# HGRN levels of a two-layer encoder: one product a chunk for both directions, with K kept as a row in use and another row

## What is computed

```python
def gates(f):                      # once for each direction
    log_f = logaddexp(log(lb), log1p(-lb) + log_sigmoid(heads(f)))
    k = (1 - lb) * sigmoid(-heads(f))
    return log_f, k

def step(state, (qc, kc, vc, lfc)):          # a chunk of a head
    b = cumsum(lfc, axis=2)
    o_inter = (qc * exp(b)) @ state
    decay = where(lower, exp(b[t] - b[s]), 0)     # for each t, s, feature
    scores = einsum('tk,sk,tsk->ts', qc, kc, decay)
    o = scores @ vc + o_inter
    state = exp(b_last) * state + (kc * exp(b_last - b)).T @ vc
```

## Time and profile before

| | |
|---|---|
| median of 3 runs | 2987.6 us (2986.75 to 2990.24) |
| the profiled execution | 2987.38 us, its span 2985.6 us |
| granted TensorE clock, mean | 0.957 of full |
| PE busy | 2762.4 us (93%) |
| DVE busy | 1412.0 us (47%) |
| HGRN levels, from the first to turn_k of the last head | 1382.96 to 2092.77 us |

### The profile page before, as it was taken

One profiled execution on the slowest core, in us unless ns is written; L12 is line 12 of the kernel. 1 busy time (PEld: TensorE's weight loads), 2 busy tenths in 40 slices (PEclk: granted clock), 3 DMA queues, 4 the chain that ended last, 5 costly groups with the idle time before them and its releaser, 6 DMA issues. The chain is left out here.

```text
span 2985.6 us, 36800 instructions
## 1 busy us (share of the span) xinstructions
PE 2762.4 (93%) x14372; PEld 2332.0 (78%) x14372; DVE 1412.0 (47%) x2483; ACT 551.4 (18%) x809; POOL 620.4 (21%) x448
## 2 busy tenths in 40 slices
PE   6686699999999999978999999999799999999996
PEld 5575577788888888767888888889678888888885
DVE  8599416533332322544555655556483332333326
ACT  3222313111111111121222222221211111111110
POOL 3868311111112111111111111110011111111120
PEclk8798799999999999989999999997899999999998
DMA  4233214111111111011101011000411111111101
GB/s 134 70 104 94 68 44 168 57 43 56 42 42 45 54 56 43 29 56 36 29 22 35 21 35 28 21 21 0 169 37 49 56 56 42 47 52 42 42 14 57
DMA packets 207704, 158.01 MB, mean 53 GB/s; under 512 B 15616, under 2 KB 189824, under 8 KB 206720
## 3 DMA queue, kind: packets, MB, share of 16 engines
q1 hardware_dynamic: 207616, 156.81, 17.2%
HBM read 139.02 MB, written 17.76 MB: 53 GB/s over the span
## 5 line engine op out<-in xcount | busy, mean ns | idle before, releaser
L588 DVE TENSOR_TENSOR h<-h,ps 128x512 f32<-128x512 f32 x320 | 219.5, 686 | 199.9 <-PE ps L365 199.6
L347 PE MATMUL ps<-aT_hi,w_hi 128*128 128x512 f32 x704 | 278.5, 396 | 3.2 <-DVE aT_lo L561 3.2
L347 PE MATMUL ps<-aT_hi,w_lo 128*128 128x512 f32 x704 | 276.4, 393 | 0.0
L347 PE MATMUL ps<-aT_lo,w_hi 128*128 128x512 f32 x704 | 274.2, 389 | 0.0
L1728 PE MATMUL ps<-aT_hi,w_hi 128*128 128x512 f32 x640 | 257.2, 402 | 1.7 <-PEq L241 1.7
L1728 PE MATMUL ps<-aT_hi,w_lo 128*128 128x512 f32 x640 | 251.3, 393 | 0.0
L1728 PE MATMUL ps<-aT_lo,w_hi 128*128 128x512 f32 x640 | 250.0, 391 | 0.0
L1762 PEld LDWEIGHTS ps<-hg_q_decayed,hg_k_decayed 128*128 128x128 f32 x1792 | 227.2, 207 | 6.2 <-DVE hg_k_decayed L2041 2.8
L1762 PE MATMUL ps<-hg_q_decayed,hg_k_decayed 128*128 128x64 f32 x1792 | 225.6, 289 | 2.6 <-DVE hg_k_decayed L2041 2.6
L1700 POOL TENSOR_TENSOR w_lo<-w_raw,w_hi 128x1024 fp32r<-128x1024 f32 x38 | 94.4, 2493 | 639.1 <-ACT w_hi L62 639.1
L571 DVE TENSOR_TENSOR s5o_act_out<-s5o_act_out,ps 128x512 f32<-128x512 f32 x44 | 30.2, 687 | 350.7 <-ACT s5o_act_out L460 350.7
(11 more groups left out here) (313 smaller groups left out, 5957.6 us busy)
## 6 DMA issues: line engine op xcount, KB each, us to landing
w_raw<-in_ffn_w_in_dram SPq DMA_DIRECT2D x44, 512.0 KB, 5.1
w_raw<-in_hg_w_in_dram SPq DMA_DIRECT2D x40, 512.0 KB, 3.9
s5o_raw<-in_ffn_w_in_dram SPq DMA_DIRECT2D x22, 512.0 KB, 5.1
s5o_raw<-in_ffn_w_out_dram SPq DMA_DIRECT2D x11, 1024.0 KB, 5.2
hgo_raw<-in_ffn_w_in_dram SPq DMA_DIRECT2D x22, 512.0 KB, 5.0
hgo_raw<-in_ffn_w_out_dram SPq DMA_DIRECT2D x11, 1024.0 KB, 5.0
h<-in_x_dram SPq DMA_DIRECT2D x4, 1024.0 KB, 8.9
s_w_raw<-in_s_w_in_dram SPq DMA_DIRECT2D x8, 512.0 KB, 4.8
```

Source lines behind the costliest of these rows:

```text
L347: ins = t.matmul(ps[:, 2 * b + a, :], w[q][:, a, kk, :], x[:, kk, rows], start=(kk == 0 and m == 0), stop=(kk == KT - 1 and m == 2))
L588: v.tensor_tensor(part, part, ps[:, 4 + m % 4, :], ALU.add).then_inc(S["out_acc"], 1)
```

## The change

`Q` of both directions becomes one tile, `q_both` (named hg_q_decayed), with the backward row first and the forward row 1024 elements behind it. `K` becomes three rows: `k_used[0]`, `k_used[1]` and `k_other`. The row in use holds, at each position, the K (forward or backward) that this level multiplies; `k_other` holds the K of the other direction at that position. One product a chunk then serves both directions: it loads the chunk of the row in use and streams 128 columns, which `q_used` gathers block by block, alternately from the backward and the forward row. The result is a full 128x128 square in natural order over banks 2 and 3.

From one level to the next half of the positions change their direction. So DVE copies the middle two of every four blocks from `k_other` into the row that comes next, and multiplies the four quarters of the row in use by their block totals, two into the next row and two into `k_other`; the last level has halves for quarters. This stands ahead of the wait for the products; then come the two Q instructions, and one masked copy of 1024 elements. PE waits for `level_moved` (Q done) and for `level_kept` (the masked copy done) before the next level. `start_k` on ACT writes in four strided instructions of 512.

```diff
-    Q = [sb(f"q_decayed{d}", [P, T]) for d in range(2)]
-    K = [sb(f"k_decayed{d}", [P, T]) for d in range(2)]
+    q_both = sb("q_decayed", [P, 2 * T + HC])
+    Q = [q_both[:, (1 - d) * T:(2 - d) * T] for d in range(2)]
+    k_used, k_other = [sb(f"k_used{b}", [P, T]) for b in range(2)], sb("k_other", [P, T])
+    K = [k_used[HLV % 2], k_other]
...
+    def q_used(lv, c):
+
+        s = 1 << lv
+        rows = q_both[:, 0:2 * (T + s)].rearrange("p (e x) -> p e x", e=2)[:, :, c * HC:(c + 1) * HC]
+        return rows.rearrange("p e (b two s) -> p b e two s", two=2, s=s)[:, :, :, 0, :]
...
-                for d in range(2):
-                    if lv:
-                        t.wait_ge(E["level_moved"], 2 * HLV * n + 2 * (lv - 1) + d + 1)
-                    for c in range(NHC):
-                        q = chunks(Q[d])[:, c, :].rearrange("p (b e s) -> p b e s", e=2, s=1 << lv)[:, :, 1 - d, :]
-                        ins = t.matmul(ps[:, 2 + d, c * (HC // 2):(c + 1) * (HC // 2)], chunks(K[d])[:, c, :], q,
-                                       start=True, stop=True)
-                    ins.then_inc(E["level_done"], 1)
+                if lv:
+                    t.wait_ge(E["level_moved"], HLV * n + lv)
+                    t.wait_ge(E["level_kept"], HLV * n + lv)
+                for c in range(NHC):
+                    ins = t.matmul(bank_rows(2)[:, c, :], k_used[lv % 2][:, c * HC:(c + 1) * HC], q_used(lv, c),
+                                   start=True, stop=True)
+                ins.then_inc(E["level_done"], 1)
...
                 for d in range(2):
-                    a.activation(K[d][:, :], k_raw[d][:, :], ACT.Copy, scale=lb[:, 1, ds(n, 1)]
-                                 ).then_inc(E["k_started"], 1)
+                    for side, to in ((d, k_used[0]), (1 - d, k_other)):
+                        a.activation(halves(to, 0, side), halves(k_raw[d], 0, side), ACT.Copy, scale=lb[:, 1, ds(n, 1)]
+                                     ).then_inc(E["k_started"], 1)
...
                 for lv in range(HLV):
+                    now, then = k_used[lv % 2], k_used[1 - lv % 2]
...
+                        passed = [a[:, :].rearrange("p (b e) -> p b e", e=4 << lv)[:, :, 1 << lv:3 << lv]
+                                  for a in (then, k_other)]
+                        v.tensor_copy(*passed).then_inc(E["k_passed"], 1)
+                    v.wait_ge(E["k_passed"], HLV * n + lv + 1)
...
+                            for e in range(2):
+                                v.tensor_tensor(quarter(then if d == e else k_other, lv, 2 * e + d),
+                                                quarter(now, lv, 2 * e + d),
+                                                bc(by[:, :, e], 2, [P, T // (4 << lv), 1 << lv]), ALU.mult)
+                    v.wait_ge(E["level_done"], HLV * n + lv + 1)
...
+                    for d in range(2):
+                        qs = halves(Q[d], lv, 1 - d)
+                        ins = v.tensor_tensor(qs, qs, bc(pair(d, lv, d), 2, [P, T // (2 << lv), 1 << lv]), ALU.mult)
+                    ins.then_inc(E["level_moved"], 1)
+                    v.copy_predicated(scores[:, :, :], bc(mask[:, lv, :], 1, [P, NHC, HC]), bank_rows(2)
+                                      ).then_inc(E["level_kept"], 1)
```

More of the change, by code:

```diff
@@ L1865, in gate @@
                 if not first(m):
[L1866 removed]
+                    a.wait_ge(E["level_moved"], HLV * (m - 1) + 1)
                     carry(a, m)
@@ L2022, in core @@
                 for lv in range(HLV):
-                    s_ = 1 << lv
-                    nb = HC // (2 * s_)
-                    for d in range(2):
[L2026 to L2030, removed]
-                        to = scores[:, :, :].rearrange("p c (b e s) -> p c b e s", e=2, s=s_)[:, :, :, 1 - d, :]
-                        mk = mask[:, lv, :].rearrange("p (b e s) -> p b e s", e=2, s=s_)[:, :, 1 - d, :]
-                        of = ps[:, 2 + d, :].rearrange("p (c b s) -> p c b s", c=NHC, s=s_)
-                        v.copy_predicated(to.rearrange("p c b s -> p (c b) s"),
-                                          bc(mk, 1, [P, NHC, nb, s_]),
-                                          of.rearrange("p c b s -> p (c b) s"))
-                        qs, ks = halves(Q[d], lv, 1 - d), halves(K[d], lv, d)
-                        full = [P, T // (2 * s_), s_]
-                        v.tensor_tensor(qs, qs, bc(pair(d, lv, d), 2, full), ALU.mult)
-                        v.tensor_tensor(ks, ks, bc(pair(d, lv, 1 - d), 2, full), ALU.mult
-                                        ).then_inc(E["level_moved"], 1)
@@ new lines, in core @@
+                    now, then = k_used[lv % 2], k_used[1 - lv % 2]
+                    if not (first(n) and lv == 0):
+                        v.wait_ge(E["level_moved"], HLV * n + lv)
+                        carry(v, n)
+                    if lv == HLV - 1:
+                        v.tensor_copy(halves(then, lv, 1), halves(k_other, lv, 1)).then_inc(E["k_passed"], 1)
+                    else:
+                        passed = [a[:, :].rearrange("p (b e) -> p b e", e=4 << lv)[:, :, 1 << lv:3 << lv]
+                                  for a in (then, k_other)]
+                        v.tensor_copy(*passed).then_inc(E["k_passed"], 1)
@@ new lines, in core @@
+                    v.wait_ge(E["k_passed"], HLV * n + lv + 1)
+                    carry(v, n)
+                    for d in range(2):
+                        by = pair(d, lv, 1 - d)
+                        if lv == HLV - 1:
+                            v.tensor_tensor(halves(k_other if d else then, lv, d), halves(now, lv, d),
+                                            bc(by, 2, [P, NHC, 1 << lv]), ALU.mult)
+                        else:
+                            by = by.rearrange("p (b e) -> p b e", e=2)
+                            for e in range(2):
+                                v.tensor_tensor(quarter(then if d == e else k_other, lv, 2 * e + d),
+                                                quarter(now, lv, 2 * e + d),
+                                                bc(by[:, :, e], 2, [P, T // (4 << lv), 1 << lv]), ALU.mult)
```

11 lines of the change are left out of this document (7 added, 4 removed).

## The result

The changed kernel takes 2918.3 us (median of 4 runs, 2917.7 to 2920.8), against 2988.8 us of the kernel before beside it: a ratio of 0.977, 95% interval 0.975 to 0.978, so it is faster. The forecast was 2917.5 us. The profiled execution took 2918.65 us, its span 2916.9 us, at a mean granted clock of 0.958.

A forecast was written before the change was run, and what follows sets the result against it. PE was taken to bound the first seven heads, while in the last PE and DVE take turns. 85.3 - 9.7 - 10.2 - 0.3 + 4.8 = 69.9 us off 2987.4 gave 2917.5 us, range 2896 to 2936.

The forecast's parts named there:

- Products on PE: Level products, first seven heads: 16 x 0.109 = 1.75 us a level, 1.74 less, 85.3 us saved over 49 levels.
- rival 2: Short runs cost: gathered products 0.218 us at levels 0 and 1, level-0 quarters 0.60; 2928 or 2940 us; chance 0.15.
- Start of heads 1 to 6: Unit 0.26 us late, level 1 1.35 late behind DVE's chain: 1.6 us a head, 9.7 us lost.
- Level 3: First seven heads: POOL's split stops DVE's quarters, so level 3 starts 1.45 us late; 10.2 us lost.
- A steady head: Median distance between levels 0 of heads 1 to 6; was to be 9.12 us shorter.
- A: Stretch from second hg_gs row ahead of head 0 to its level 0; ACT's K start costs 0.3 us once.
- The last head: Level 1 2.3 us later, then 6.21 us a level against 6.87 at the low clock: 4.8 us gained.
- The alternative of 15 us: Last head at the full clock: 4.52 us a level, gain 15.0 us instead of 4.8.
- 1: POOL's split stops nothing, or the last head gets full clock: 2907 us for one, 2897 for both; chance 0.22.
- 3: DVE's masked copy takes 2.4 us instead of 1.24 at every level: 2940 us; chance 0.07.
- 4: Nothing gained: gathered products take 0.218 us at every level, levels keep 3.49; about 2984 us; chance 0.02.
- 5: Slower: jumping between two rows costs products more than 0.218 us; at 0.327, 3080 us; chance 0.04.

The follow-up runs named there:

- l0_plain: Changed kernel with level 0 streaming 128 neighbouring columns of one row instead of gathering from two rows (scores differ): 2919.4 us, ratio 0.977.
- no_split2: Changed kernel with POOL's weight split beside level 2 covering one of eight parts: 2909.5 us, ratio 0.973.
- keepq: Changed kernel with `keep_q` moved behind the K work of the next level: 2910.3 us, ratio 0.974.
- warm: Changed kernel with unread 512-column products filling PE's gaps in the last head: 2910.0 us, ratio 0.974.
- earlyk: Changed kernel with the K work of level 0 done a head ahead, behind `k_sum`: 2913.9 us, ratio 0.975.
- best: Changed kernel with two more PSUM banks, `keep_q` behind K work, level-0 K work a head ahead except the first head's, last-head fillers: 2887.5 us, ratio 0.966.
- after: The changed kernel itself, with no further edit: 2918.3 us, ratio 0.977 to the kernel before.
- best_cold: The same kernel as best but without the fillers in the last head: 2892.2 us, ratio 0.967.

## Why the prediction came out

The sum was 69.9 us; the ruler gives 69.25. Point by point:

- **Products on PE** (85.3): right in kind, a little too large. Levels 2 to 6 save 3.49 - 1.70 = 1.79 us, more than the 1.74 taken (level 3, behind its wait, 1.71). Level 1 saves 1.58 and level 0 only 0.96: rival 2's first half is half true. The gathered product costs 0.158, between the two bounds 0.109 and 0.218. Seven levels save 11.4 a steady head instead of 12.2.
- **Start of heads 1 to 6** (1.6 a head): the chain as forecast put level 1 at 8.96 after level 0, and it stands at 9.38. The K copy and its wait were too dear by 0.27 (0.58 from copy to quarter, forecast 0.85), the quarters too cheap by 0.74 (2.10 for four, forecast 1.36): rival 2's other half, one element in four costs. The wait reads 1.06 instead of 1.35 only because PE itself was later. l0_plain shows that the dear products cost nothing in these heads, and 0.9 us once in the first: the two misses overlap, they don't add.
- **Level 3** (1.45 a head): cause and place as forecast, shown by no_split2 and keepq; the size was 1.15. I let all four quarters stand behind POOL. The first was under way, was stopped, and ended 0.3 us behind POOL; three were left. Level 3 comes 8.38 after level 2, forecast 8.80.
- **A steady head** was to be 9.12 us shorter and is 9.04 (94.52 to 85.48): +0.42 at the start, +0.15 at level 1, -0.42 at level 3, and a beat of 7.29 for 7.35 on the other levels. Part of the good agreement is that misses of opposite sign met.
- **The first head** was to gain 10.7 us (no late start) and gained 9.30. Its level 0 ran mostly at the low clock in this profile (granted 0.63 over 1380 to 1390, 0.82 before) and took 3.43 us against 3.84 before. This term was missing, and it changes from run to run: in warm, whose edit lies in the last head alone, the clock there was 0.91, level 0 took 2.62 us, and the head gained 10.84.
- **A** was to lose 0.3 (ACT) and gained 1.2: POOL's two splits fell on `k_sum` (3.40 us) and Q (4.50) instead of the gate totals (6.83 before, 2.58 now). The stop is as long, but `k_sum` is done 2.1 us sooner, and PE's diagonal product, which waits for `k_sum`, now runs beside Q; before, level 0 stood behind it. ACT's four instructions took 0.5 us more than the two, and POOL began 4.58 us into A instead of 4.07, just behind the last of the gate totals: the term that was to cost 0.3 seems to have turned the order and so to have gained. None of it was foreseen, no run tests it, and it makes up for the 1.4 us missing in the first head by luck.
- **The last head** (4.8): 4.18. Low clock as taken but for one level, 6.43 a level instead of 6.21 (and one of 5.71), and 9.02 to level 1 instead of 8.58 (the quarters again). The alternative of 15 us stood at the right place: with fillers C gains 13.1 on the kernel before.
- **Rivals.** 1 did not happen, though warm and no_split2 show that each half was there to be had: 8.9 us in C, and 7.6 at level 3. 2 came in part, at level 0 in product and quarter, and still cost 0.4 us a head at level 1 instead of 1.04, since the K copy was cheaper than taken. 3 is out (1.34 us at every level). 4 and 5 are out: level 2 takes 1.70.

## To carry to other kernels

Where PE is bound by the number of float32 matmul and weight-load pairs, halve the pairs and let a longer moving side carry the work, but follow what the relieved engine now asks of its partner: here one wait for room in PSUM cost some 22 us, and two more banks took it away. When a wait appears beside a stop by another engine, the order of the work before the stop can be as good a cure as removing the stop (2910.3 against 2909.5 us here). Before a small difference between two runs is put down to an edit, compare their granted clocks over the same stretch. Compare variants over the stretch they edit, from a mark ahead of it, since the rest of the program moved by more than the effects in dispute.

## What the runs showed of the hardware

- A moving operand gathered one element from each of two rows in turn cost 0.158 us for 128 columns, against 0.106 in runs of four and more and 0.114 in runs of two (level 1 without a wait, in earlyk: 1565.14 to its unit at 1566.97); for 64 columns the same gather cost nothing (3.70 for 32, against 3.69). Whether the single elements or the change of row cost was not taken apart. The Trainium skill (Advanced Engine Details and Errata, "SBUF Cachelines") says that at least two hits on a 16-byte line are needed, and that a different line at each access pays; for 128 columns the trace agrees, with 1.5 times at one hit, and shows 1.1 at two, which by the page are enough.
- A DVE product of 256 elements, one in four, cost 0.53 us, one behind the other, against 0.33 at runs of four; a plain copy of 512 elements inside SBUF took 0.42 to 0.43, what 256 take in a product. The Trainium skill (VectorE: DVE Perf Modes, "Mode 2×_2P") gives a copy inside SBUF two results a cycle, and a product of two tensors not: the trace agrees, and the copy at level 0 (0.43, two of every four elements) shows no penalty.
- Which of DVE's instructions meets POOL's split is settled by hundredths of a microsecond: in best `k_sum` began with POOL at 1375.22 and took 1.22, in after it began 0.02 behind POOL and took 3.40.
- The last head, at a granted 0.50 over 2000 to 2010 in after, stood at 1.00 in warm, where unread products of 512 columns filled its gaps, with no cost elsewhere to be seen. Without them the clock can be high too: 1.00 over 1965 to 1975 in best_cold, with PE busy for 7.23 of these 10 us.
